# Second quads of three output projections: one 512-column matmul for the high and low parts of the input

## The chip, the cores and the metric

The kernel runs on one core of a Trainium2 chip. The metric is the device time of one execution in microseconds (us). The kernel before takes 906.71 us, the median of three runs between 906.47 and 907.17.

## The reference, cut to what matters

Two blocks of a network work on 256 tokens of width 1024, in float32. The parts that matter here:

```python
h = h + even_mixer(rmsnorm(h), ...)        # ends in concatenate([y_a, y_b]) @ w_out    (even_out)
h = h + conv_ffn(rmsnorm(h), ...)          # up0, down0
h = h + odd_mixer(rmsnorm(h), ...)         # attention, ends in y @ w_out               (qkv0, out0)
h = h + conv_ffn(rmsnorm(h), ...)          # up1, down1
h = rmsnorm(h)
h = h + mix @ w_o                          # mix: two kinds of attention                (qkv1, out1)
h = h + (gelu(gate) * val) @ w_down        # up2, down2
h = h + sigmoid(xn @ w_ple_gate) * (p @ w_ple_proj)                                   # ple
return rmsnorm(h)
```

The three output projections are products of a 256 x 1024 input with a 1024 x 1024 weight matrix, and the result is added to the residual h. Each is followed by a norm and the up projection of a feed-forward part.

## The kernel before, in words

Everything is kept transposed: 128 channels lie on the partitions, and the 256 tokens are columns. The residual `h` is 8 chunks of 128 x 256. A product in float32 accuracy is made from float32r parts: each weight w is split into a high part `wh` (w rounded, by ScalarE, line 578) and a low part `wl` (w minus `wh`, by VectorE at line 974 or GpSimd at line 516), each input x likewise into two parts that lie side by side, in `xs` (from a norm) or `ys` (from a mixer or an activation), 256 columns each. The product is wh x_high + wh x_low + wl x_high.

**Units and quads.** A unit is 128 output channels: 8 tiles of 128 x 128 weights (11 in the down phases), loaded by a DMA of SyncE into one of four slots of `raw` (line 453), rounded, split, multiplied into one of four PSUM banks `proj[:, s]`, and read out. Four units are a quad. The phases (line 59) go through their quads in order; the three output projections `even_out`, `out0` and `out1` have two quads each, so 8 units for the 8 chunks of `h`. Line 93 numbers all quads through, and semaphores count units over the whole program: `units_done` (a unit's sum is finished), `bank_read` (it is read), `hi_ready` and `lo_ready[s]` (weights rounded and split). ScalarE rounds the unit that is one quad ahead when the unit that held its slot is done (line 577). For `out0` and `out1` the weights of the first three units of the second quad are prepared early, in free room of `ys` (`early_units`, line 131, found through `split_weights`, line 393).

**Two ways to multiply on TensorE.** `unit` (line 542) issues three matmuls of 256 columns for each tile, all three into the same 256 columns of the bank; here this is called a narrow tile. `wide_unit` (line 519) issues one matmul of `wh` with both input parts, 512 columns, and one of `wl` with the high part, 256 columns, added to the second half of the bank; here a wide tile. The two halves of the bank must then be added. The up and down phases use wide tiles. `both_ys` gives both parts of `ys`, `from_ys` the two separately. All output projections use narrow tiles: their first quad is written out by hand, interleaved with the end of the mixer (lines 1840 to 1875, and 1947 and 1948), their second quad is `out_rest` (line 1621).

**The out phase on the other engines.** `residual_out` on VectorE (line 1146) does for each unit, in this order: wait for the unit, add it to its chunk of `h` (line 1154), split the weights of the unit one quad ahead (line 974), make the low part of the next norm's input (`norm_low`, line 990, after ScalarE has made the high part) and add the chunk's squares to a sum (`add_square`, line 998). For the last unit the split comes last. ScalarE's `residual_out` (line 693) rounds weights, waits for `bank_read`, and makes the high part of the norm's input (line 600) and the squares (line 595). Its `norm_root` (line 606) follows with a table load (line 607) and the root (line 614). `residual_down` on VectorE (line 1166) is the like for wide units: two additions for each unit (lines 1177 and 1178), the first inside `steps(...)`, which makes VectorE wait for its own instruction to be complete before it goes on.

**The phase behind.** `from_norm` (line 1599) starts the up phase on TensorE: seven tiles of the first unit, each waiting for its chunk's low part (`xl_ready`), seven of the second unit, then the eighth of both, the matmul of the statistics (line 1587), and the rest. So TensorE starts the next phase before the last chunk of the norm's input is there. The engines execute their own instructions in order.

Of the kernel before, what the change touches and what calls it, by code (L numbers as in the profile page):

```python
# [29 lines left out]
SEQ = 256  # L30
# [9 lines left out]
RING = 4  # L40
SLOT = HALF * P
# [46 lines left out]
def build_program(nc, streams, x_in, p_in, vectors_in, pool_in, gate_in, rel_in, onehot_in, count_in, out):  # L88
    f32, f32r = mybir.dt.float32, mybir.dt.float32r
    ALU, ACT, AX = mybir.AluOpType, mybir.ActivationFunctionType, mybir.AxisListType  # L90
    ds = bass.ds

    base, total = {}, 0
# [4 lines left out]
    quads_of = {name: quads for name, quads, _ in PHASES}  # L98
# [34 lines left out]
    def is_early(name, i, s):  # L133

        return isinstance(i, int) and (base[name] + i + 1, s) in early_units
# [10 lines left out]
    def final_unit(name, i, s):  # L146

        return isinstance(i, int) and i == quads_of[name] - 1 and s == RING - 1
# [4 lines left out]
    with ExitStack() as ctx:  # L153
        def sb(name, shape, dt=f32):
            return ctx.enter_context(nc.sbuf_tensor(name, shape, dt))

        def sem(name):
            return ctx.enter_context(nc.semaphore(name))

        h = sb("h", [P, DC, SEQ])  # L160
# [4 lines left out]
        wh = sb("wh", [P, RING, SLOT], f32r)  # L165
        wl = sb("wl", [P, RING, SLOT], f32r)
# [80 lines left out]
        proj, aux = psum[:, 0:RING, :], psum[:, RING:2 * RING, :]  # L247
# [33 lines left out]
        def squares(n, parity):  # L281

            if n == 7:
                return last_square[:, parity:parity + 1, :]
            bank = (2 if n % 2 == 0 else RING) + parity
            return psum[:, bank:bank + 1, 0:SEQ]
# [20 lines left out]
        units_done = sem("units_done")  # L307
        bank_read = sem("bank_read")
# [84 lines left out]
        def split_weights(q, s, width):  # L393

            if isinstance(q, int) and (q, s) in early_units:
                at = PAIRS * 2 * SEQ + s * 2 * DC * P
                return flat_ys[:, at:at + DC * P], flat_ys[:, at + DC * P:at + 2 * DC * P]
            return wh[:, s, 0:width], wl[:, s, 0:width]

        def unit_bank(name, i, s):  # L400

            if name == "out1" and isinstance(i, int) and i == 0 and s == RING - 1:
                return spare_bank
            return proj[:, s:s + 1, 0:SEQ]
# [6 lines left out]
        def each_quad(engine, first, end, body, steps=None, per_quad=0):  # L411


            if end - first < 2:
                for i in range(first, end):
                    body(i)
                return
            begun = steps.n if steps else 0
            with engine.Fori(first, end) as i:
                if steps:  # L420
                    steps.base, steps.n = (i - first) * per_quad + begun, 0
                body(i)
                if steps:
                    assert steps.n == per_quad, steps.n
            if steps:
                steps.base, steps.n = 0, begun + per_quad * (end - first)
# [540 lines left out]
        def _(dve):  # L967
            steps = Steps(dve, dve_step)
# [7 lines left out]
            def split_ahead(name, i, s):  # L976

                target, q = ahead(name, i, s)
                if target and s not in pool_slots(target, q):
                    split_unit(q, s, tiles_of[target])  # L980

            def phase(name, body, per_quad=0):
                last = quads_of[name] - 1
                each_quad(dve, 0, last, lambda i: body(i), steps, per_quad)
                body(last)

            def norm_low(n, m):

                dve.wait_ge(xh_ready, m + (DC * n + 1))
                nc.vector.scalar_tensor_tensor(xs[:, ds(m, 1), 1, :], h[:, ds(m, 1), :], column(VECTORS[n][0], m),  # L990
                                               xs[:, ds(m, 1), 0, :].bitcast(f32), ALU.mult, ALU.subtract).then_inc(xl_ready, 1)

            def add_square(n, m, parity):
                dve.wait_ge(square_ready, m + (DC * n + 1))
                dve.wait_ge(square_used, m + DC * n)
                if n == MID:
                    nc.vector.tensor_tensor(mid_acc[:, :], mid_acc[:, :], mid_square[:, parity, :], ALU.add)
                nc.vector.tensor_tensor(acc[:, :], acc[:, :], squares(n, parity)[:, 0, :], ALU.add).then_inc(square_used, 1)
# [67 lines left out]
            for padded, width in ((pool_u, PAD), (pool_a, PAD), (pool_b, PAD), (even_cv, TAPS - 1)):  # L1066
                last = nc.vector.memset(padded[:, 0:width], 0.0)
# [75 lines left out]
            def clear_acc():  # L1143
                steps(nc.vector.memset(acc[:, :], 0.0))

            def residual_out(name, n):
                clear_acc()

                def body(i):
                    q = i + base[name]  # L1150
                    for s in range(RING):
                        m = i * RING + s
                        dve.wait_ge(units_done, q * RING + s + 1)
                        nc.vector.tensor_tensor(h[:, ds(m, 1), :], h[:, ds(m, 1), :], unit_bank(name, i, s), ALU.add)\
                          .then_inc(bank_read, 1)
                        final = final_unit(name, i, s)
                        if not final and not is_early(name, i, s):
                            split_ahead(name, i, s)
                        dve.wait_ge(bank_read, q * RING + s + 1)
                        norm_low(n, m)  # L1160
                        add_square(n, m, s % 2)
                        if final:
                            split_ahead(name, i, s)
                phase(name, body)
# [328 lines left out]
            for i in range(quads_of["ple"]):  # L1493
                q = i + base["ple"]
                for s in range(RING):
                    m = i * RING + s
# [21 lines left out]
        def _(pe):  # L1518
            def wide_unit(q, s, inputs, tiles, start=True, stop=True, ready=None, read=None, bank=None):


                bank = proj[:, s if bank is None else bank, :]
                if tiles[0] == 0:
                    pe.wait_ge(lo_ready[s], q + 1)
                    if start and read is not None:
                        pe.wait_ge(bank_read, read)
                for n, t in enumerate(tiles):
                    if ready:
                        ready(t)
                    first, last = start and n == 0, stop and n == len(tiles) - 1  # L1530
                    w = slice(t * P, (t + 1) * P)
                    nc.tensor.matmul(bank, wh[:, s, w], inputs(t), start=first, stop=False)  # L1532
                    done = nc.tensor.matmul(bank[:, SEQ:2 * SEQ], wl[:, s, w], inputs(t)[:, 0, :], start=False, stop=last)  # L1533
                return done

            def both_xs(t):
# [24 lines left out]
            ALL = range(DC)  # L1561

            def slot_read(q, s):

                return None if isinstance(q, int) and q == 0 else q * RING + s - 3
# [9 lines left out]
            def slot_bank(s):  # L1575
                return proj[:, s, 0:SEQ]
# [15 lines left out]
            def quad_of(name, inputs):  # L1592
                def quad(i, slots=range(RING)):
                    q = i + base[name]
                    for s in slots:
                        unit(q, s, slot_bank(s), inputs, ALL, read=slot_read(q, s)).then_inc(units_done, 1)
                return quad
# [21 lines left out]
                each_quad(pe, 1, quads_of[name], quad)  # L1619

            def out_rest(name):
                each_quad(pe, 1, quads_of[name], quad_of(name, from_ys))

            def down_phase(name, ys_name):

# [14 lines left out]
            def attention(layer, name, out_name, n_norm):  # L1640
# [233 lines left out]
                for s in range(RING):  # L1874
                    out_unit(s, range(DC - 1, DC), start=False).then_inc(units_done, 1)
                out_rest(out_name)

            def tables():
# [49 lines left out]
            for j in range(1, quads_of["even_in"]):  # L1928
                for s in range(RING):
                    read = slot_read(j, s)  # L1930
                    if s == 0:

                        pe.wait_ge(pooled_in, j)
                        read = None
                    elif (j, s) == (1, 1):
                        pe.wait_ge(conv_copied, 1)
                        read = None
# [7 lines left out]
            q = base["even_out"]  # L1945
# [17 lines left out]
            for i in range(quads_of["ple"]):  # L1963
                q = i + base["ple"]
                for s in range(RING):
# [4 lines left out]
                    for t in range(PLE):  # L1970
                        w = slice((DC + t) * P, (DC + t + 1) * P)
# [18 lines left out]
            for b in range(2):  # L1990
                last = nc.tensor.matmul(last_stat[:, b:b + 1], squares(7, 1)[:, 0, b * P:(b + 1) * P], ones[:, 0:1], start=False, stop=True,
                                        skip_group_check=True)
# [3 lines left out]
            for b in range(2):  # L1996
                last = nc.tensor.matmul(last_rows[:, b * P:(b + 1) * P], last_rstd[:, b:b + 1].to_broadcast([P, P]), ident[:, :],
                                        start=True, stop=True)
# [106 lines left out]
```

## Time and profile before

| | us |
|---|---|
| median of 3 runs | 906.71 |
| lowest and highest | 906.47, 907.17 |
| the profiled execution | 907.1 |
| its span, first to last instruction | 905.4 |
| TensorE busy | 898.6 |
| VectorE busy | 670.1 |
| ScalarE busy | 572.1 |
| GpSimd busy | 243.6 |

The profile is of one execution. PE is TensorE's matmuls and PEld its weight loads, DVE is VectorE, ACT is ScalarE, POOL is GpSimd. An engine is busy while it executes at least one instruction; matmuls overlap in TensorE's pipeline, so the durations of single matmuls add up to more than its busy time. Idle time of an engine is put down to the instruction that ended it. The mean granted clock of TensorE over the span is 0.999 of full speed.

### The profile page before, as it was taken

Reading aid. Unit: us, or ns where it says so; the run is one execution under the profiler, and the core shown is the slowest. Engines: PE = TensorE matmul, PEld = TensorE weight load, DVE = VectorE, ACT = ScalarE, POOL = GpSimd, SP = SyncE. Lnnn points to the kernel's source line nnn. Section 1 sums busy time; section 2 is a strip of 40 time slices with the busy share of each in tenths; the row PEclk is TensorE's granted clock in tenths of the full one; section 3 lists DMA queues with packets and bytes.
Section 4 is the critical chain, followed back from the end, with each engine's and each line's share of the span. In section 5 each row is a group of like instructions: output and inputs, shape, how many; then the busy total and the mean of one; then the engine's idle time right before and its main releaser. Section 6 shows DMA issues by size and latency. Waiting matters only on the chain.

```text
span 905.4 us, 18274 instructions
## 1 busy us (share of the span) xinstructions
PE 898.6 (99%) x6022; PEld 814.0 (90%) x6022; DVE 670.1 (74%) x1353; ACT 572.1 (63%) x996; POOL 243.6 (27%) x130
## 2 busy tenths in 40 slices
PE   9999999999999999999999999999999999999997
PEld 8999888888898999988888888999998888888897
DVE  8987887786657756678777866788667766686566
ACT  7456776774445556577666644667658877774453
POOL 0421444420000002044443000070104988850000
PEclk9999999999999999999999999999999999999999
DMA  8545677677534434456666654444335655576521
GB/s 307 196 167 163 210 236 238 210 225 268 173 130 140 139 129 153 162 167 210 231 193 212 230 190 147 127 154 141 119 122 179 211 190 192 192 236 208 185 96 47
DMA packets 47193, 163.51 MB, mean 181 GB/s; under 512 B 5234, under 2 KB 10098, under 8 KB 47141
## 3 DMA queue, kind: packets, MB, share of 16 engines
q1 hardware_dynamic: 42336, 158.12, 53.5%
q10 hardware_dynamic: 4805, 4.70, 1.6%
q8 instruction: 32, 0.52, 0.3%
q14 instruction: 20, 0.16, 0.1%
HBM read 161.71 MB, written 3.44 MB: 182 GB/s over the span
## 4 chain that ended last, share of the span: by engine, by line
PE 95%; DVE 2%; ACT 1%; issue 1%; DVEq 0%
PE psum L1532 41%; PE psum L1533 20%; PE psum L1556 7%; PE psum L1557 7%; PE psum L1558 7%; PE psum L1679 2%; PE psum L1681 2%; PE psum L1682 2%; PE psum L1792 1%; PE psum L1894 1%; PE psum L1767 1%; PE psum L1731 1%; PE psum L1729 1%; ACT wh L578 1%; PE psum L1905 0%
## 5 line engine op out<-in xcount | busy, mean ns | idle before, releaser
L578 ACT ACTIVATE wh<-raw 128x1024 fp32r<-128x1024 f32 (+2 forms) x266 | 297.1, 1119 | 116.4 <-PE psum L1533 80.6
L1532 PE MATMUL psum<-xs,wh 128*128 128x512 f32 x1056 | 367.2, 394 | 0.0
L516 POOL TENSOR_TENSOR wl<-raw,wh 128x1024 fp32r<-128x1024 f32 (+1 forms) x86 | 209.5, 2440 | 450.7 <-ACT wh L578 449.3
L1533 PE MATMUL psum<-xs,wl 128*128 128x256 f32 x1056 | 292.7, 277 | 0.0
L974 DVE TENSOR_TENSOR wl<-raw,wh 128x1024 fp32r<-128x1024 f32 (+2 forms) x180 | 241.3, 1345 | 52.3 <-ACT wh L578 52.0
L1532 PEld LDWEIGHTS psum<-xs,wh 128*128 128x128 f32 x1056 | 198.0, 188 | 45.9
L1533 PEld LDWEIGHTS psum<-xs,wl 128*128 128x128 f32 x1056 | 198.3, 188 | 0.1
L1532 PE MATMUL psum<-ys,wh 128*128 128x512 f32 x528 | 183.2, 394 | 0.0
L1533 PE MATMUL psum<-ys,wl 128*128 128x256 f32 x528 | 146.3, 277 | 0.0
L1556 PE MATMUL psum<-xs,wh 128*128 128x256 f32 x416 | 120.3, 289 | 0.0
L1532 PEld LDWEIGHTS psum<-ys,wh 128*128 128x128 f32 x528 | 99.0, 188 | 23.0
L1558 PE MATMUL psum<-xs,wl 128*128 128x256 f32 x416 | 117.6, 283 | 0.0
L1557 PE MATMUL psum<-xs,wh 128*128 128x256 f32 x416 | 117.6, 283 | 0.0
L1031 DVE SCALAR_TENSOR_TENSOR psum<-work,vec,psum 128x256 f32<-128x256 f32 x184 | 88.7, 482 | 23.7 <-ACT psum L732 23.3
L1533 PEld LDWEIGHTS psum<-ys,wl 128*128 128x128 f32 x528 | 99.1, 188 | 0.0
L1023 DVE TENSOR_TENSOR psum<-psum,work 128x256 f32<-128x256 f32 x132 | 56.6, 429 | 40.8 <-ACT work L729 40.6
L729 ACT ACTIVATE work<-psum 128x256 f32<-128x256 f32 x132 | 50.4, 382 | 51.1 <-PE psum L1533 50.8
L1556 PEld LDWEIGHTS psum<-xs,wh 128*128 128x128 f32 x416 | 79.6, 191 | 1.6 <-issue 1.4
L1557 PEld LDWEIGHTS psum<-xs,wh 128*128 128x128 f32 x416 | 79.7, 192 | 0.1
L1558 PEld LDWEIGHTS psum<-xs,wl 128*128 128x128 f32 x416 | 79.6, 191 | 0.0
L732 ACT ACTIVATE psum<-work,vec 128x256 f32<-128x256 f32 x88 | 50.1, 569 | 36.7 <-DVE work L1014 33.7
L1014 DVE TENSOR_TENSOR work<-psum,rstd 128x256 f32<-128x256 f32 x100 | 42.1, 421 | 5.2
(239 smaller groups left out, 1230.3 us busy)
## 6 DMA issues: line engine op xcount, KB each, us to landing
raw<-in_up SPq DMA_DIRECT2D x132, 512.0 KB, 3.3
raw<-in_down SPq DMA_DIRECT2D x48, 704.0 KB, 4.2
raw<-in_qkv SPq DMA_DIRECT2D x48, 512.0 KB, 3.3
raw<-in_out SPq DMA_DIRECT2D x16, 512.0 KB, 3.4
raw<-in_even_in SPq DMA_DIRECT2D x12, 512.0 KB, 3.6
raw<-in_ple SPq DMA_DIRECT2D x8, 640.0 KB, 3.8
raw<-in_even_out SPq DMA_DIRECT2D x8, 512.0 KB, 3.6
raw<-in_even_in SPq DMA_DIRECT2D x8, 256.0 KB, 5.2
```

The lines of the kernel that those rows point to most:

```text
L516: nc.gpsimd.tensor_tensor(low, raw[:, s, 0:tiles * P], high.bitcast(f32), ALU.subtract)\
L578: nc.scalar.activation(split_weights(q, s, tiles * P)[0], raw[:, s, 0:tiles * P], ACT.Copy).then_inc(hi_ready, 1)
L729: nc.scalar.activation(high_sums[:, s % 2, :], proj[:, s, 0:SEQ], ACT.Copy).then_inc(high_copied, 1)
L732: nc.scalar.activation(target, padded[:, 2:2 + SEQ], ACT.Identity, bias=column(bias_name, chunk), scale=column(taps, chunk + 2 * chunks)). ...
L974: nc.vector.tensor_tensor(low, raw[:, s, 0:tiles * P], high.bitcast(f32), ALU.subtract).then_inc(lo_ready[s], 1)
L1023: return nc.vector.tensor_tensor(proj[:, s, 0:SEQ], proj[:, s, SEQ:2 * SEQ], high_sums[:, s % 2, :], ALU.add)
L1031: return nc.vector.scalar_tensor_tensor(out_ap, padded[:, k:k + SEQ], column(taps, chunk + k * chunks), out_ap, ALU.mult, ALU.add)
L1532: nc.tensor.matmul(bank, wh[:, s, w], inputs(t), start=first, stop=False)
L1533: done = nc.tensor.matmul(bank[:, SEQ:2 * SEQ], wl[:, s, w], inputs(t)[:, 0, :], start=False, stop=last)
L1556: nc.tensor.matmul(bank, high_w[:, w], high, start=first, stop=False)
L1557: nc.tensor.matmul(bank, high_w[:, w], low, start=False, stop=False)
L1558: done = nc.tensor.matmul(bank, low_w[:, w], high, start=False, stop=last)
```

## The change

The second quad of each output projection is computed by `wide_unit` with `both_ys`, in place of `unit` with `from_ys`: per tile one matmul of 512 columns and one of 256 in place of three of 256. `wide_unit` now takes its weights through `split_weights`, so that it finds those that were prepared early. On VectorE the addition of each unit of the second quad (`i == 1`) becomes two: the first half of the bank, a wait for that addition through `steps`, then the second half; `bank_read` is raised by the second. The first quads stay as they were.

```diff
--- before.py
+++ after.py
@@ -1151,8 +1151,12 @@
                     for s in range(RING):
                         m = i * RING + s
                         dve.wait_ge(units_done, q * RING + s + 1)
-                        nc.vector.tensor_tensor(h[:, ds(m, 1), :], h[:, ds(m, 1), :], unit_bank(name, i, s), ALU.add)\
-                          .then_inc(bank_read, 1)
+                        added = nc.vector.tensor_tensor(h[:, ds(m, 1), :], h[:, ds(m, 1), :], unit_bank(name, i, s), ALU.add)
+                        if isinstance(i, int) and i == 1:
+
+                            steps(added)
+                            added = nc.vector.tensor_tensor(h[:, ds(m, 1), :], h[:, ds(m, 1), :], proj[:, s:s + 1, SEQ:2 * SEQ], ALU.add)
+                        added.then_inc(bank_read, 1)
                         final = final_unit(name, i, s)
                         if not final and not is_early(name, i, s):
                             split_ahead(name, i, s)
@@ -1524,13 +1528,14 @@
                     pe.wait_ge(lo_ready[s], q + 1)
                     if start and read is not None:
                         pe.wait_ge(bank_read, read)
+                high_w, low_w = split_weights(q, s, SLOT)
                 for n, t in enumerate(tiles):
                     if ready:
                         ready(t)
                     first, last = start and n == 0, stop and n == len(tiles) - 1
                     w = slice(t * P, (t + 1) * P)
-                    nc.tensor.matmul(bank, wh[:, s, w], inputs(t), start=first, stop=False)
-                    done = nc.tensor.matmul(bank[:, SEQ:2 * SEQ], wl[:, s, w], inputs(t)[:, 0, :], start=False, stop=last)
+                    nc.tensor.matmul(bank, high_w[:, w], inputs(t), start=first, stop=False)
+                    done = nc.tensor.matmul(bank[:, SEQ:2 * SEQ], low_w[:, w], inputs(t)[:, 0, :], start=False, stop=last)
                 return done
 
             def both_xs(t):
@@ -1619,7 +1624,9 @@
                 each_quad(pe, 1, quads_of[name], quad)
 
             def out_rest(name):
-                each_quad(pe, 1, quads_of[name], quad_of(name, from_ys))
+                q = base[name] + 1
+                for s in range(RING):
+                    wide_unit(q, s, both_ys, ALL, read=slot_read(q, s)).then_inc(units_done, 1)
 
             def down_phase(name, ys_name):
```

## Rows read from the trace of the kernel before

**Rows 1.** The page: busy time by engine, granted clock by slice, chain by engine.

```profile
PE 898.6 (99%) x6022; PEld 814.0 (90%) x6022; DVE 670.1 (74%) x1353; ACT 572.1 (63%) x996; POOL 243.6 (27%) x130
...
PEclk9999999999999999999999999999999999999999
...
PE 95%; DVE 2%; ACT 1%; issue 1%; DVEq 0%
```

**Rows 2.** Timeline of TensorE in even_out; columns: start us, us, engine, line, instruction.

```profile
56.10 0.28 PE L1556 MATMUL psum<-ys,wh 128*128 128x256 f32 x1
...
79.02 0.19 PEld L1532 LDWEIGHTS psum<-xs,wh 128*128 128x128 f32 x1
...
79.14 0.40 PE L1532 MATMUL psum<-xs,wh 128*128 128x512 f32 x1
```

**Rows 3.** Timeline of TensorE at the start of up1.

```profile
380.69 0.40 PE L1532 MATMUL psum<-xs,wh 128*128 128x512 f32 x1
...
382.81 0.40 PE L1532 MATMUL psum<-xs,wh 128*128 128x512 f32 x1
...
386.34 0.59 PE L1587 MATMUL psum<-acc,ones 128*128 128x256 f32 x2
```

**Rows 4.** Line 1533 in down0: duration ns min/median/max, first and last start.

```profile
L1533 PE MATMUL psum<-ys,wl x176: 274/277/280, 201.9 to 262.6; 128*128 128x256 f32 x176
```

**Rows 5.** Timeline of VectorE in out0, second quad.

```profile
376.10 0.41 DVE L1154 TENSOR_TENSOR h<-h,psum 128x256 f32<-128x256 f32 x1
...
376.43 1.22 DVE L974 TENSOR_TENSOR wl<-raw,wh 128x1024 fp32r<-128x1024 f32 x1
...
378.29 0.41 DVE L1154 TENSOR_TENSOR h<-h,psum 128x256 f32<-128x256 f32 x1
...
380.49 0.41 DVE L1154 TENSOR_TENSOR h<-h,psum 128x256 f32<-128x256 f32 x1
...
381.95 0.47 DVE L990 SCALAR_TENSOR_TENSOR xs<-h,vec,xs 128x256 fp32r<-128x256 f32 x1
...
382.68 0.41 DVE L1154 TENSOR_TENSOR h<-h,psum 128x256 f32<-128x256 f32 x1
...
383.74 0.48 DVE L990 SCALAR_TENSOR_TENSOR xs<-h,vec,xs 128x256 fp32r<-128x256 f32 x1 [0.65 <-ACT xs L600]
```

**Rows 6.** Timeline of VectorE and TensorE at the start of up2.

```profile
682.32 0.40 PE L1532 MATMUL psum<-xs,wh 128*128 128x512 f32 x1
...
683.76 0.48 DVE L990 SCALAR_TENSOR_TENSOR xs<-h,vec,xs 128x256 fp32r<-128x256 f32 x1
...
684.45 0.40 PE L1532 MATMUL psum<-xs,wh 128*128 128x512 f32 x1
```

**Rows 7.** Timeline of VectorE in even_out, third unit of the second quad.

```profile
77.61 1.23 DVE L974 TENSOR_TENSOR wl<-raw,wh 128x1024 fp32r<-128x1024 f32 x1 [0.60 <-ACT wh L578]
...
78.75 0.48 DVE L990 SCALAR_TENSOR_TENSOR xs<-h,vec,xs 128x256 fp32r<-128x256 f32 x1
```

**Rows 8.** Timeline of VectorE in the down phases, first and last of 24 pairs.

```profile
213.51 0.41 DVE L1177 TENSOR_TENSOR h<-h,psum 128x256 f32 x1
214.03 0.42 DVE L1178 TENSOR_TENSOR h<-h,psum 128x256 f32 x1
...
866.11 0.42 DVE L1177 TENSOR_TENSOR h<-h,psum 128x256 f32<-128x256 f32 x1 [0.23 <-PE psum L1533]
866.63 0.42 DVE L1178 TENSOR_TENSOR h<-h,psum 128x256 f32<-128x256 f32 x1
```

**Rows 9.** Timeline at the end: TensorE released by VectorE.

```profile
896.47 0.42 DVE L998 TENSOR_TENSOR acc<-acc,work 128x256 f32<-128x256 f32 x1
...
896.95 0.52 PEld L1986 LDWEIGHTS psum<-ones,acc 128*128 128x128 f32 x4 [0.53 <-DVE acc L998]
```

**Rows 10.** Timeline of ScalarE at the start of up1.

```profile
384.91 1.28 ACT L607 ACT_TABLE_LOAD   x1
...
386.97 0.48 ACT L614 ACTIVATE work<-psum,eps 128x256 f32<-128x256 f32 x1 [0.78 <-PE psum L1587]
```

## The prediction

> **What bounds the kernel now.** I read the page first. TensorE is busy for 99% of the span, and the chain that ended last is 95% TensorE [rows 1]. Time is therefore saved by giving TensorE less to do, and lost by whatever makes it wait; work on another engine costs nothing until TensorE waits for it. The durations of single matmuls (0.28 us for 256 columns, 0.40 for 512 [rows 2]) overlap each other, so they can't be summed. I went to the timeline of TensorE for the pace from start to start. A narrow tile is three matmuls of 256 columns: the 64 tiles of even_out start at 56.10 and end at 79.14 us [rows 2], which is 23.04 / 64 = 0.360 us per tile. A wide tile is one matmul of 512 columns and one of 256. The 16 wide tiles that follow directly on narrow ones in up1 run from 380.69 to 386.34 us, 5.65 / 16 = 0.353 us per tile [rows 3]; the 176 wide tiles of down0 run at (262.6 - 201.9) / 175 = 0.347 us [rows 4].
>
> Then I read VectorE around the same places, since the change gives it more to do. In out0 the residual additions of the second quad start at 376.10, 378.29, 380.49 and 382.68 us [rows 5]: 2.19 us apart, back to back, with no idle time, while TensorE delivers a unit every 8 x 0.360 = 2.88 us. VectorE came into this quad behind. TensorE had finished the last unit when up1 began, at 380.69 [rows 3], and VectorE took it up at 382.68, 2.0 us late.
>
> **What TensorE waits for next** is the order of up1: it takes tiles 0 to 6 of its first unit at once, and each tile wants the low part of that chunk of the norm (line 990). Tile 6 wants chunk 6, which comes from the third unit of the out quad. Its low part ends at 381.95 + 0.47 = 382.42, and TensorE starts tile 6 at 382.81 [rows 3, 5]: a margin of 0.39 us. In out1 it ends at 683.76 + 0.48 = 684.24 and tile 6 starts at 684.45 [rows 6]: 0.21 us. In even_out it ends at 78.75 + 0.48 = 79.23, and tile 6 is due at 79.14 + 6 x 0.353 = 81.26 [rows 2, 7]: 2.03 us.
>
> **What the change removes.** 96 tiles (8 tiles x 4 units x 3 projections) go from three matmuls to two. If they run at the pace of wide tiles that follow narrow ones, each saves 0.360 - 0.353 = 0.007 us: 0.22 us per projection, 0.66 in all. If they run at down0's pace, 0.013 us each: 0.42 per projection, 1.25 in all, and the first 16 tiles of each up phase may then keep that pace too, another 3 x 16 x 0.006 = 0.3. The bounds of the gain are thus 0.66 and 1.55 us. I take the low one, since the second quads follow directly on a narrow first quad, as at the start of up1 [rows 3].
> TensorE's clock is granted in full, 2.4 GHz, in every slice of the span [rows 1], so the clock gives nothing back. The Trainium skill (TensorE: Matmul & The Clock Gate, section Back-to-back issue gap) puts a warm matmul at its columns over 2.4 GHz plus about 2.5 ns. By that rule an estimate would be 327.5 ns for a narrow tile and 325 for a wide one, 2.5 ns saved each, 0.24 us in all. The trace doesn't agree: its tiles take 360 and 347 to 353 ns.
>
> **What it adds.** 12 additions on VectorE, four in each second quad. The nearest rows are the two additions of the down phases, which have the same operands and the same wait between them: 213.51 to 214.03 and 866.11 to 866.63 us [rows 8]. All 24 such pairs start 0.51 to 0.53 us apart. The wait for the engine's own step lets the first one (0.42 us) drain. So each unit grows by 0.52 us, from 2.19 to 2.71. The lower bound is 0.33 us, the distance from an addition to the next independent instruction (376.10 to 376.43 [rows 5]). Behind this wait stand the split of the next phase's unit, the low part of the norm, the sum of squares and the next unit's addition; ScalarE's norm work waits for the same counter, bank_read, which now rises after the second addition. No DMA, no split and no rounding is moved. The waits for weights are far off: the split of up1's first unit is done at 376.43 + 1.22 = 377.65, 3 us before TensorE wants it [rows 3, 5].
>
> **Where it lands.** Three additions stand ahead of chunk 6: 3 x 0.52 = 1.56 us.
> In out0 VectorE has no idle time between them to absorb any of it. The low part of chunk 6 ends at 382.42 + 1.56 = 383.98. TensorE, restarted by a semaphore, loads weights 0.06 us after the releasing instruction ends (896.47 + 0.42 = 896.89 to 896.95 [rows 9]) and starts its matmul 0.12 us after the load begins (79.02 to 79.14 [rows 2]). Tile 6 starts at 383.98 + 0.18 = 384.16 instead of 382.81: **1.35 us lost**. The 0.22 us saved in this quad only makes TensorE arrive earlier and wait longer.
> In out1: 684.24 + 1.56 + 0.18 = 685.98 instead of 684.45: **1.53 us lost**, the saving swallowed as before.
> In even_out there are 2.03 us of margin less 0.22, and VectorE is idle for 0.60 us in the unit of chunk 6, waiting for ScalarE's weights [rows 7], which takes up part of the 1.56. No wait: **0.22 us saved**.
> The last chunk has one addition more. In out0 its low part started at 383.74 and took 0.48 [rows 5]; it now ends at 384.22 + 4 x 0.52 = 386.30. TensorE has 8 tiles left from 384.16 before it wants it, until 384.16 + 8 x 0.35 = 386.96: no second wait. The statistics matmul moves from 386.34 to 387.69 with TensorE; ScalarE's table load, in line behind chunk 7, ends at 384.91 + 1.28 + 2.08 = 388.27, and the root that started 0.63 us after the statistics (386.97) is due at 388.32 [rows 3, 10]. It is just in time, and I cost it at nothing.
> Sum: 1.35 + 1.53 - 0.22 = +2.66 us. The profiled execution was 907.1 us with a span of 905.4, 0.4 us above the median of 906.71, so it would be 909.8, and the median about 909.3 us. Low end: additions at 0.33 us (0.57 less in out0 and in out1), the fast pace in even_out (0.2) and in the up tiles (0.3) leave about +1.0, 907.7. High end: a second wait of some tenths behind the late last chunk or the late root in each of the two, about +3.7, 910.4. Both ends lie above the time before.
>
> **The rivals.**
> A. *VectorE has room, so TensorE's saving is all that shows.* For it: 2.71 us per unit is still less than the 2.82 (8 x 0.353) that TensorE takes, and VectorE is idle for a quarter of the span [rows 1]. The point from which it decides is the low part of chunk 6, at TensorE's arrival less 0.18 us. If VectorE kept up there, nothing would be lost and 0.66 to 1.55 us saved: about 905.6 us. Against it: the margins of 0.39 and 0.21 us are smaller than a single addition, and VectorE enters the quad behind and without idle time. Chance 0.07. This gain can't reach 0.2%.
> B. *The wait comes, but the additions cost little.* At about 0.33 us each with the fast pace everywhere the loss is some 1 us: 907.7 us. For it: the second addition could overlap the first more than in down. Against it: 24 pairs say otherwise. Chance 0.15.
> C. *The last chunk or the root becomes a second wait.* With 0.05 us of margin at the root and 0.66 at the last chunk, ScalarE's longer line behind chunk 7 could hold the first banks of up1 and up2. TensorE writes these again about 5 us later, so most is hidden; 0.5 us each would give 910.3 us. Chance 0.08.
> That the change doesn't do what it says can hardly be: the second quad is written out with a constant index, so the branch with the second addition is taken.
>
> **How the numbers follow.** The forecast, a wait at tile 6 in out0 and out1 and none in even_out, has 0.70. A measurement of this kernel can tell about 0.2%, 1.8 us, from no change: slower means over 908.5 us, faster under 904.9. The forecast at 909.3 lies above that line, but with some spread; nearly nine tenths of its 0.70 are past it, all of C too; A and B are within 0.2%. I give slower 0.70, same 0.27, faster 0.03. The range 907.6 to 910.4 leaves out A and a little at each end.
>
> **What would show it.** In the profile of the changed kernel: in out0 and out1 TensorE idle for about 1.5 us ahead of the seventh tile of the first up unit, released by line 990's instruction on VectorE, and none in even_out; the additions of the second quads 2.71 us apart in out0 and out1; two starts 0.52 us apart within each; 32 wide tiles in about 11.3 us in each second quad (at the fast pace 11.1). Wrong would be: no gap at tile 6, a gap in even_out, or a gap at the last tile or at the banks of the second up quad.

## The result, and the profile after

The changed kernel takes 910.86 us (median of 6 runs, 910.60 to 912.14), the kernel before 906.79 us in the same comparison. The ratio is 1.0047, with a 95% interval from 1.0034 to 1.0059: slower, and slower than the top of the predicted range by 0.46 us. The profiled execution (910.63 us) has a span of 908.9 us, 3.5 us more than before. The medians differ by 4.07 us; the other 0.5 us is that the profiled execution of before (907.1 us) lay 0.3 above its median and that of the changed kernel 0.2 below. All that follows explains the 3.5.

The page of the changed kernel, its span, its busy times and its chain by engine:

```profile
span 908.9 us, 18094 instructions
...
PE 898.4 (99%) x5926; PEld 813.2 (89%) x5926; DVE 674.7 (74%) x1365; ACT 572.2 (63%) x996; POOL 244.3 (27%) x130
...
PE 90%; DVE 5%; ACT 2%; issue 2%; DMA 1%; SPq 0%; DVEq 0%; ACTq 0%
```

TensorE is busy for 0.2 us less than in [rows 1] and the span is 3.5 us longer: what came on top is time in which TensorE is idle, within the program or at its start and end. The chain is no longer 95% TensorE, since it now passes through VectorE and the first loads. To see where the time lies, I compared the same points of both timelines of TensorE. First the changed kernel: the first wide tile of even_out, the statistics of up0, tile 6 and the statistics of up1, the same two of up2, and the last matmuls (columns: start us, us, engine, line, instruction, idle time before it and what ended it):

```profile
68.27 0.40 PE L1537 MATMUL psum<-ys,wh 128*128 128x512 f32 x1
...
85.23 0.59 PE L1592 MATMUL psum<-acc,ones 128*128 128x256 f32 x2
...
384.30 0.49 PE L1537 MATMUL psum<-xs,wh 128*128 128x512 f32 x1 [1.08 <-DVE xs L990]
...
384.75 0.40 PE L1537 MATMUL psum<-xs,wh 128*128 128x512 f32 x1
...
387.88 0.38 PE L1592 MATMUL psum<-acc,ones 128*128 128x256 f32 x1
...
687.21 0.49 PE L1537 MATMUL psum<-xs,wh 128*128 128x512 f32 x1 [1.26 <-DVE xs L990]
...
690.78 0.38 PE L1592 MATMUL psum<-acc,ones 128*128 128x256 f32 x1
...
902.21 0.68 PE L2004 MATMUL psum<-ident,last_rstd 128*128 128x128 f32 x4
```

The kernel before at the same points that [rows 3] doesn't hold: the first statistics, those of up0 and up2, and the last matmuls:

```profile
19.20 0.60 PE L1587 MATMUL psum<-acc,ones 128*128 128x256 f32 x2
...
84.79 0.38 PE L1587 MATMUL psum<-acc,ones 128*128 128x256 f32 x1
...
687.98 0.38 PE L1587 MATMUL psum<-acc,ones 128*128 128x256 f32 x1
...
899.42 0.69 PE L1997 MATMUL psum<-ident,last_rstd 128*128 128x128 f32 x4
```

| stretch | before us | after us | difference |
|---|---|---|---|
| start to the first statistics | 19.20 | 19.85 | +0.65 |
| to the statistics of up0 | 65.59 | 65.38 | -0.21 |
| to the statistics of up1 (wait at tile 6) | 301.55 | 302.65 | +1.10 |
| to the statistics of up2 (wait at tile 6) | 301.64 | 302.90 | +1.26 |
| to the last matmuls | 211.44 | 211.43 | -0.01 |
| to the end of the span | 5.98 | 6.69 | +0.71 |
| sum | 905.4 | 908.9 | +3.5 |

The differences at up0, up1 and up2 are those that were predicted, as -0.22, +1.35 and +1.53. Start and end, together 1.36 us, were not in the forecast at all.

**The two waits.** The waits of TensorE put them down to the instruction that was named (columns: waited for, us in total, times, longest):

```profile
PE psum L1537 <- DVE xs L990: 2.3, 2, 1.3
```

The timeline of VectorE in out0, to be laid beside [rows 5]: the two additions of the fifth unit, its split, the next two units' first additions, and chunk 6's low part:

```profile
376.55 0.41 DVE L1154 TENSOR_TENSOR h<-h,psum 128x256 f32<-128x256 f32 x1
...
377.00 0.42 DVE L1158 TENSOR_TENSOR h<-h,psum 128x256 f32<-128x256 f32 x1
...
377.34 1.22 DVE L974 TENSOR_TENSOR wl<-raw,wh 128x1024 fp32r<-128x1024 f32 x1
...
379.20 0.41 DVE L1154 TENSOR_TENSOR h<-h,psum 128x256 f32<-128x256 f32 x1
...
381.85 0.41 DVE L1154 TENSOR_TENSOR h<-h,psum 128x256 f32<-128x256 f32 x1
...
383.77 0.48 DVE L990 SCALAR_TENSOR_TENSOR xs<-h,vec,xs 128x256 fp32r<-128x256 f32 x1
```

The units are 2.65 us apart (376.55, 379.20, 381.85), not the 2.19 of before. The second addition starts 0.45 us behind the first, where 0.52 was expected from [rows 8]. The low part of chunk 6 ends at 383.77 + 0.48 = 384.25, and TensorE takes tile 6 at 384.30, 0.05 us later and not 0.18. Both terms were somewhat too large: 3 x 0.07 + 0.13 = 0.34 us. The first tile behind a wait takes 0.45 us to the next start (384.30 to 384.75), 0.10 more than usual, and the nine tiles after it run at (387.88 - 384.75) / 9 = 0.348 us, the fast pace, which gives half of that back.

ScalarE at the start of up1, to be laid beside [rows 10]: the table load ends at 388.46 and the root starts at 388.51, 0.63 us behind the statistics at 387.88, so it is in time, as the prediction had it.

```profile
387.18 1.28 ACT L607 ACT_TABLE_LOAD   x1
...
388.51 0.47 ACT L614 ACTIVATE work<-psum,eps 128x256 f32<-128x256 f32 x1
```

**The start.** ScalarE's first instruction waits for a small DMA of scale vectors. In the kernel before it starts at 3.95 us:

```profile
3.95 0.91 ACT L624 ACTIVATE xs<-h,vec 128x256 fp32r<-128x256 f32 x2 [0.41 <-DMA vec<-in_vectors]
```

In the changed kernel it waits 1.6 us longer, and the first statistics follow 0.65 us later than before. It is not this load alone: the first weights (`raw<-in_even_in`, 256 KB each) take 6.9 us from issue to landing in the page of the changed kernel, 5.2 in that of before.

```profile
5.54 0.91 ACT L624 ACTIVATE xs<-h,vec 128x256 fp32r<-128x256 f32 x2 [2.00 <-DMA vec<-in_vectors]
...
19.85 0.38 PE L1592 MATMUL psum<-acc,ones 128*128 128x256 f32 x1
```

**The end.** The DMA view of the last microseconds, of the kernel before and of the changed one (columns: what, times, KB each, median us from issue to landing):

```profile
out<-h SPq DMA_DIRECT2D x3, 256.0 KB, 2.1
...
out<-h SPq DMA_DIRECT2D x2, 128.0 KB, 1.9
```

```profile
out<-h SPq DMA_DIRECT2D x3, 256.0 KB, 2.7
...
out<-h SPq DMA_DIRECT2D x2, 128.0 KB, 2.0
```

VectorE's last instructions and the stores' issues keep their places relative to the last matmuls (0.45 us from one to the other in both), but the larger stores take 2.7 us to land in place of 2.1. Nothing in the diff touches a load or a store. The page of before lists 32 packets on queue q8, whose kind is "instruction"; the changed kernel has one fewer:

```profile
q8 instruction: 31, 0.51, 0.2%
```

These packets don't stand in the way of the first loads themselves: in the DMA views of both kernels and of experiment 8 none of them falls in the first 12 us. The number is used below only as a mark of how long the program is.

### The profile page after: what moved, and what is told of

Same layout as the page of the kernel before. It is cut to its first block, busy times and chain, and to the rows that moved or that the text cites. A ratio compares the mean times of both kernels' runs of the same rounds, so it can differ in the third digit from the quotient of the medians.

```text
span 908.9 us, 18094 instructions
## 1 busy us (share of the span) xinstructions
PE 898.4 (99%) x5926; PEld 813.2 (89%) x5926; DVE 674.7 (74%) x1365; ACT 572.2 (63%) x996; POOL 244.3 (27%) x130
## 4 chain that ended last, share of the span: by engine, by line
PE 90%; DVE 5%; ACT 2%; issue 2%; DMA 1%; SPq 0%; DVEq 0%; ACTq 0%
PE psum L1537 40%; PE psum L1538 21%; PE psum L1561 6%; PE psum L1562 6%; PE psum L1563 6%; PE psum L1686 2%; PE psum L1688 2%; PE psum L1689 2%; PE psum L1799 1%; DVE wl L974 1%; ACT wh L578 1%; DMA h<-in_x 1%; PE psum L1774 1%; DVE acc L998 1%; PE psum L1738 1%
## 5 line engine op out<-in xcount | busy, mean ns | idle before, releaser
L1537 PE MATMUL psum<-ys,wh 128*128 128x512 f32 x576 | 200.3, 392 | 0.0
L1538 PE MATMUL psum<-ys,wl 128*128 128x256 f32 x576 | 161.6, 281 | 0.0
L1537 PEld LDWEIGHTS psum<-ys,wh 128*128 128x128 f32 x576 | 107.9, 187 | 23.6
L1538 PEld LDWEIGHTS psum<-ys,wl 128*128 128x128 f32 x576 | 109.1, 189 | 0.0
L600 ACT ACTIVATE xs<-h,vec 128x256 fp32r<-128x256 f32 (+1 forms) x48 | 24.4, 508 | 34.3 <-DVE h L1158 13.6
```

The source lines that it names most:

```text
L1537: nc.tensor.matmul(bank, high_w[:, w], inputs(t), start=first, stop=False)
L1538: done = nc.tensor.matmul(bank[:, SEQ:2 * SEQ], low_w[:, w], inputs(t)[:, 0, :], start=False, stop=last)
```

## The experiments

**Theory T:** the additions on VectorE, which starts the second quad behind, make tile 6 late, as predicted; start and end are slower because TensorE's program has become shorter and its code lies otherwise. **Rivals:** start and end vary from execution to execution; the wide matmuls or the use of both halves of a bank cause them; or the second quads are too slow on VectorE whatever happens in the first. In this section "the middle" is the time from the first statistics to the last matmuls, read in each timeline as above: 880.22 us before, 882.36 changed.

**1 and 2. Both kernels again, unchanged.**

> The changed kernel, unchanged. Of the 3.5 us by which its span is longer, its trace shows 0.65 us ahead of the first statistics, -0.21 in even_out, +1.10 at up1's tile 6, +1.26 at up2's, and 0.70 behind the last matmuls. Theory (the waits at tile 6 are the change, start and end are the execution's): 909 to 911 us, and the waits again 1.0 to 1.3 us, while start and end differ from the first profile by some tenths. Rival (the changed program starts and ends later every time): start and end as in the first profile, 910.9 us.

> The kernel before, unchanged, for a second look at its start and end. Theory: 906.8 us, with the first statistics matmul within a few tenths of 19.2 to 19.85 us in either kernel. Rival (start and end belong to the program): first statistics at 19.20 us and the last matmuls to the end of the span as in the first profile.

Measured: the changed kernel 910.73 us, the kernel before 906.62. First statistics at 19.79 and 19.34 us, the middle 882.39 and 880.25, the end 6.7 and 5.9 us behind the last matmuls. So the slow start and end are the program's and come again. The rival of c_after was right, and my expectation that they would differ by tenths was wrong.

**3. One addition only.**

```diff
-                        if isinstance(i, int) and i == 1:
-                            steps(added)
-                            added = nc.vector.tensor_tensor(h[:, ds(m, 1), :], h[:, ds(m, 1), :], proj[:, s:s + 1, SEQ:2 * SEQ], ALU.add)
```

> The changed matmuls with the first of the two additions alone: the low parts' sum, the second half of the bank, is left out of the residual in the second quads. Theory (the additions make the waits): no wait at tile 6 in up1 and up2 or one of some hundredths, 0.66 us less than before at the slow pace, 906.1 us, plus what start and end give (up to 1.4). Rival (the wide matmuls themselves delay something, their banks or their clock): still 1.5 us or more above before at tile 6.

Measured: 908.16 us (ratio 1.0016, 1.0007 to 1.0024). The middle is 879.72 us, 0.50 less than before: without the second addition nothing is lost, and the wide matmuls save somewhat less than the 0.66 that was expected of their slow pace. Yet the kernel is slower than before. In the profiled execution its first statistics come at 21.21 us, and its stores land late as in the changed kernel:

```profile
out<-h SPq DMA_DIRECT2D x3, 256.0 KB, 2.8
```

The start is worse than that of the changed kernel because TensorE was granted only half of its clock for a while. Before that it had waited 1.06 us for a small load; in the changed kernel that wait is 0.2 us. This execution took 909.41 us, 1.25 more than the median, which suggests that the lowered clock belongs to it and not to most executions. (The second line is the window from 8 to 10 us: us, busy time and count of PE, PEld, DVE, ACT and POOL, granted clock, DMA share, GB/s.)

```profile
6.73 1.03 PE L1884 MATMUL psum<-qkv 33*18 33x512 f32 x2 [1.06 <-DMA qkv<-in_rel]
...
8.00:10.00 2.00, 1.75 (x8) 1.76 (x9) 1.91 (x5) 1.58 (x4) 0.00 (x0) 0.50 1.05 395
```

**4. The additions alone, on the narrow kernel.**

```diff
-                        nc.vector.tensor_tensor(h[:, ds(m, 1), :], h[:, ds(m, 1), :], unit_bank(name, i, s), ALU.add)\
-                          .then_inc(bank_read, 1)
+                        added = nc.vector.tensor_tensor(h[:, ds(m, 1), :], h[:, ds(m, 1), :], unit_bank(name, i, s), ALU.add)
+                        if isinstance(i, int) and i == 1:
+                            steps(added)
+                            added = nc.vector.tensor_tensor(h[:, ds(m, 1), :], h[:, ds(m, 1), :], unit_bank(name, i, s), ALU.add)
+                        added.then_inc(bank_read, 1)
```

> The matmuls of the kernel before, but the first half of the bank is added a second time in the second quads, with the same wait between (so the residual gets the sum twice there). Theory: up1's and up2's tile 6 start at the same point behind VectorE as in the changed kernel, 1.1 and 1.3 us late, and even_out saves nothing: 2.4 us above before, 909.2 us. Rival (the additions alone are hidden): within 0.5 us of before.

Measured: 909.32 us, ratio 1.0027 (1.0017 to 1.0037), as T expected. The middle is 882.64 us, 2.42 above before; start (19.31) and end (5.9 us) are those of before. The waits of TensorE:

```profile
PE psum L1535 <- DVE xs L990: 1.9, 2, 1.1
```

They are 0.2 us shorter for each than in the changed kernel, since narrow tiles bring TensorE to tile 6 later. So the two waits come from the additions alone, and start and end do not.

**5. Two narrow matmuls per tile.** The product with the input's low part is left out in the second quads; no tile is wide.

```diff
 def out_rest(name):
-    each_quad(pe, 1, quads_of[name], quad_of(name, from_ys))
...
+    for t in ALL:
+        nc.tensor.matmul(slot_bank(s), high_w[:, w], ys[:, t, 0, :], start=t == 0, stop=False)
+        last = nc.tensor.matmul(slot_bank(s), low_w[:, w], ys[:, t, 0, :], start=False, stop=t == DC - 1)
```

> The kernel before with two narrow matmuls for each tile of the second quads (the product with the input's low part is left out there): 96 instructions pairs fewer, as in the changed kernel, but none wide. If the length of the program makes the slow start and end: first statistics later than 19.4 us and the end more than 6.3 us behind the last matmul. If the wide matmuls or the halves of the bank do: 19.2 to 19.35 and 5.9 to 6.0 us. TensorE saves up to 11.5 us in the second quads and VectorE then binds there.

Measured (a single execution): 907.2 us, first statistics at 20.11 us, the end 6.7 us behind the last matmuls, 31 packets on q8. A shorter program without wide matmuls has the slow start and end too; so neither the wide matmuls nor the bank halves are needed for them. The middle is only 1.57 us shorter than before although TensorE's work is 11.5 us less: it now waits for VectorE in all three places.

**6. A float32 matmul ahead of the wide quads.**

```diff
 q = base[name] + 1
+nc.tensor.matmul(psum[:, 7, 0:P], ones[:, :], ones[:, :], start=True, stop=True)
 for s in range(RING):
```

> The changed kernel with one float32 matmul of 128 columns ahead of each wide second quad. In both kernels wide tiles run at 0.353 us behind narrow ones and at 0.347 behind the float32 matmuls of the statistics. If such a matmul is what ends the slower pace: the 32 tiles of the second quad take 11.1 us in place of 11.3. If it is the statistics' place or the phase: 11.3 us as before.

Measured (a single execution): 912.43 us, most of the difference to the changed kernel at the start (21.43 us, with the granted clock at 0.50 between 10 and 12 us) and 0.2 in the middle. TensorE's timeline at the start of even_out's second quad:

```profile
69.85 0.39 PE L1628 MATMUL psum<-ones 128*128 128x128 f32 x2
...
69.99 0.48 PE L1537 MATMUL psum<-ys,wh 128*128 128x512 f32 x1
...
70.42 0.39 PE L1537 MATMUL psum<-ys,wh 128*128 128x512 f32 x1
...
70.77 0.40 PE L1537 MATMUL psum<-ys,wh 128*128 128x512 f32 x1
...
71.13 0.40 PE L1537 MATMUL psum<-ys,wh 128*128 128x512 f32 x1
...
71.48 0.40 PE L1537 MATMUL psum<-ys,wh 128*128 128x512 f32 x1
```

After the first tile the starts are again 0.35 to 0.36 us apart, and the second half of the quad runs at 0.353. So a float32 matmul by itself does not end the slow pace, although it comes with a first tile of 0.43 us, much like the one behind a wait.

**7. 96 small matmuls at the end of TensorE's program.**

```diff
 last.then_inc(last_spread, 1)
+for _ in range(96):
+    nc.tensor.matmul(proj[:, 0, 0:32], wh[:, 0, 0:P], xs[:, 0, 0, 0:32], start=True, stop=True)
```

> The changed kernel with 96 small matmuls added behind everything that TensorE has to do, so that its program holds as many instructions as before. Theory (the first loads and the last stores are slower because the program got shorter and lies otherwise): first statistics back at 19.2 to 19.35 us, end of the span 5.9 to 6.0 us behind the last needed matmul, 1.3 to 1.4 us less than the changed kernel, 909.4 us. Rival (start and end go with something else in the change): start at 19.8 us, 910.8 us.

Measured: 920.47 us, not the 909.4 that T expected. The 96 matmuls took 18.3 us, far longer than the stores that they were to hide behind, so this total and this end say nothing. The start does: first statistics at 19.35 us, ScalarE's first instruction at 3.93, 32 packets on q8, as before the change.

**8. 192 waits that are always satisfied.**

```diff
+def filler(t):
+    for _ in range(2):
+        pe.wait_ge(ones_ready, 1)
-wide_unit(q, s, both_ys, ALL, read=slot_read(q, s)).then_inc(units_done, 1)
+wide_unit(q, s, both_ys, ALL, ready=filler, read=slot_read(q, s)).then_inc(units_done, 1)
```

> The changed kernel with two waits that are always satisfied ahead of each wide tile of the second quads, 192 in all, to bring TensorE's program back to about its former length without giving the engine work. If the length makes the slow start and end: first statistics at 19.2 to 19.4 us, the end of the span 5.9 to 6.0 us behind the last matmul, the waits at tile 6 unchanged, 909.0 to 909.5 us. If not: 910.8 us. If the waits themselves slow the wide tiles, it shows as more than 11.4 us for a second quad.

Measured: 909.03 us, ratio 1.0024 (1.0014 to 1.0034). The middle is 882.51 us, within 0.15 of the changed kernel. The stores and queue q8 are those of before, and the start is back too; the first statistics come even 0.4 us earlier than the 19.20 of before:

```profile
3.89 0.91 ACT L624 ACTIVATE xs<-h,vec 128x256 fp32r<-128x256 f32 x2 [0.35 <-DMA vec<-in_vectors]
...
18.81 0.38 PE L1592 MATMUL psum<-acc,ones 128*128 128x256 f32 x1
```

```profile
out<-h SPq DMA_DIRECT2D x3, 256.0 KB, 2.1
```

```profile
q8 instruction: 32, 0.52, 0.2%
```

The same work in a longer program is 1.8 us faster. 909.03 is also near the 909.3 of the prediction, which had left start and end alone.

**9. One satisfied wait ahead of each tile, in place of two** (against experiment 8).

```diff
-    for _ in range(2):
+    for _ in range(1):
```

> The changed kernel with one satisfied wait ahead of each wide tile of the second quads in place of two, 96 in all, so half of the missing length. If start and end go with the length by degrees: first statistics near 19.4 us, the last stores half as late, 909.9 us. If it is a step (how the program lies): either like the changed kernel, 19.8 us or more and 910.8 us, or like the one with 192 waits, 18.8 to 19.3 us and 909.0 us.

Measured: 910.74 us, first statistics at 19.95 us, the larger stores 2.8 us to landing, the end 6.7 us behind the last matmuls:

```profile
q8 instruction: 31, 0.51, 0.2%
```

The expectation calls this half of the missing length. The pages don't bear that out; these are their first lines for experiments 8 and 9:

```profile
span 907.3 us, 18190 instructions
...
span 909.0 us, 18094 instructions
```

The changed kernel has 18094 instructions too. So 192 waits added 96 instructions, and 96 waits added none: of two waits ahead of a tile only one counts as an instruction of its own. Experiment 9 therefore didn't test half the length. It is a control: satisfied waits that make the program no longer leave start and end as slow as they were. Whether the effect of the length is a step or a slope stays open. No profile lies between the two groups: the seven with 18190 instructions or more have 32 packets on q8 and their first statistics at 18.8 to 19.4 us, the seven with 18106 or fewer have 31 and 19.8 to 21.4. For a step speaks that 96 added instructions brought back the whole start and end, where the page counts 96 matmuls and 96 weight loads fewer than before; but how many instructions of the program these are isn't shown.

**10. VectorE adds a unit ahead in the first quads of out0 and out1,** on the changed kernel. The body of the addition becomes `add_unit(s)`:

```diff
+begun = isinstance(i, int) and i == 0 and name != "even_out"
+if begun:
+    add_unit(0)
 for s in range(RING):
     m = i * RING + s
+    if not begun:
+        add_unit(s)
+    elif s < RING - 1:
+        add_unit(s + 1)
     final = final_unit(name, i, s)
```

> The changed kernel, and in the first quads of out0 and out1 VectorE adds a unit to the residual ahead of the norm of the unit before, in place of waiting 0.65 us for ScalarE each time. Theory (the backlog from the first quad is what makes the additions late): VectorE reaches the fifth unit some 1.7 us earlier, no wait at tile 6 in up1 and up2, 0.66 us less than before between the first statistics and the last matmuls, 907.5 to 908.2 us with start and end as in the changed kernel. Rival (the second quad itself is too slow for VectorE): waits of 1 us and more remain, 910 us.

Measured: 907.94 us, ratio 1.0014 (1.0005 to 1.0023). No wait at tile 6; the middle is 879.29 us, 0.93 less than before. That is 0.27 more than expected, which isn't explained; 0.51 of the 0.93 lie in the stretch to the statistics of up2. What is left above the kernel before is the start and the end (6.7 us). The profiled execution (908.86 us, 0.9 above the median) has its first statistics at 21.11 us, again with a lowered clock behind a wait of 1.2 us for the same small load.

**11. The same order on the kernel before.**

> The kernel before with the additions of the first quads of out0 and out1 a unit ahead, nothing else. TensorE does not wait there, so it should give nothing: 906.8 us, with VectorE at the fifth unit of out0 1.7 us earlier. More than 0.5 us either way would mean that the order on VectorE acts elsewhere too.

Measured: 906.79 us, ratio 0.9998 (0.9989 to 1.0007), the middle 880.25 us. Counted from the first statistics, VectorE reaches the fifth unit of out0 1.8 us earlier (1.7 expected), but TensorE wasn't waiting there, and it gives nothing.

**12. Both remedies on the changed kernel:** the addition a unit ahead, and the 192 satisfied waits.

> The same filling on the kernel whose first quads of out0 and out1 add a unit ahead. If the change is worth its 0.22 us per projection once VectorE's backlog and the program's length are both dealt with: no wait at tile 6, 0.6 to 0.8 us below before, 906.0 to 906.3 us. If one of them remains: 907 us and more.

Measured: 906.01 us (905.79 to 906.73), beside 906.85 for the kernel before: ratio 0.9991, interval 0.9982 to 1.0000. The middle is 879.58 us, 0.64 less than before. VectorE in the first quad of out0, with its residual additions and low parts, and the fifth unit:

```profile
369.80 0.41 DVE L1154 TENSOR_TENSOR h<-h,psum 128x256 f32<-128x256 f32 x1
...
370.13 0.48 DVE L990 SCALAR_TENSOR_TENSOR xs<-h,vec,xs 128x256 fp32r<-128x256 f32 x1
...
370.86 0.41 DVE L1154 TENSOR_TENSOR h<-h,psum 128x256 f32<-128x256 f32 x1
...
371.19 0.48 DVE L990 SCALAR_TENSOR_TENSOR xs<-h,vec,xs 128x256 fp32r<-128x256 f32 x1
...
373.92 0.41 DVE L1154 TENSOR_TENSOR h<-h,psum 128x256 f32<-128x256 f32 x1
```

From the second unit on, additions and low parts now follow each other without a wait for ScalarE. Counted from the first statistics, the fifth unit starts at 373.92 - 19.03 = 354.89 us, in place of 376.10 - 19.20 = 356.90: 2.0 us earlier, 0.2 of them from even_out. TensorE at tile 6, tile 7 and the statistics of up1:

```profile
382.57 0.40 PE L1547 MATMUL psum<-xs,wh 128*128 128x512 f32 x1
...
382.93 0.40 PE L1547 MATMUL psum<-xs,wh 128*128 128x512 f32 x1
...
385.76 0.59 PE L1602 MATMUL psum<-acc,ones 128*128 128x256 f32 x2
```

There is no gap. This is the only version with the wide second quads that isn't slower than the kernel before. The gain of 0.8 us in the medians is at the edge of what the measurement can tell.

## Why the prediction was wrong, point by point

**The saving on TensorE: right.** 32 wide tiles that follow narrow ones keep the slow pace of 0.353 us, and even_out gained 0.21 us (0.22 forecast). In out0 and out1 nothing of it shows. The rule that the prediction took from the Trainium skill (TensorE: Matmul & The Clock Gate, section Back-to-back issue gap) is given there for a single isolated matmul, and not for a stream of weight loads and matmuls as here; its estimate for even_out would be 0.08 us. The trace goes with the rows and not with it.

**The waits at tile 6: right in place, number and cause, a little too large.** Forecast 1.35 and 1.53 us, measured 1.10 and 1.26. The term for one addition was 0.52 us from the down phases and measured 0.45; the restart of TensorE was 0.18 and measured 0.05. Experiments 3 and 4 take the two parts of the change apart, and only the additions bring the waits. Experiment 10 shows what they rest on: VectorE's idle time in the first quad, 0.65 us per unit in which it waits for ScalarE. The prediction saw the backlog that comes of it, but not where it comes from.

**even_out without a wait, the last chunk and the root in time: right.** No gap appears in any of these places. Rival C didn't happen, nor did A and B.

**Start and end: this is the step that failed.** The sum of the prediction, "1.35 + 1.53 - 0.22 = +2.66 us", was put straight on the time of the whole kernel, with the words "No DMA, no split and no rounding is moved". That start and end stay as they are was assumed and had no term and no bound. They cost 0.65 + 0.71 = 1.36 us in the profile. With the wait terms at their measured size the sum is +2.15, and 2.15 + 1.36 = 3.5 us is the span's difference. The direction was right; the range, whose top stood at 910.4, had no room for this. Shown is that they go with the length of TensorE's program and not with the work in it: the changed kernel with 96 more instructions that do nothing (experiment 8) has both as before, and with 96 small matmuls at its end (7) the start too; waits that add no instruction change nothing (9), and a shorter program without wide matmuls has both slow (5). How the length reaches the first loads and the last stores isn't shown. The number of instruction packets goes with it in every profile, but it may just count the length; the placing of code or buffers in memory was not tried apart from it.

## What to carry to other kernels

An engine that the page shows idle for a quarter of the time can still be the one that is late: before moving work onto it, look at where it is behind, take the margin of the next thing that waits for it, and compare it with the added work that stands ahead. Here the margins were 0.39 and 0.21 us and the added work 3 x 0.45 = 1.35. If the backlog comes from idle time further up, reordering there (adding a unit ahead) takes the loss away: here the 2.4 us of the two waits at tile 6, where the change itself saves 0.6 us. Without the change the reordering gave nothing (experiment 11). And where less than half a per cent is at stake, a change of the program's length is a change too: compare the first and the last microseconds of both traces, and keep a term for them in the range.

## What the runs showed that was not expected

- First loads and last stores depend on the length of a program that doesn't contain them. The first small load was waited for until 3.9 to 4.0 us in all profiles with 32 packets on the instruction queue and until 5.1 to 6.0 us in all with 31; the larger stores landed in 2.1 us in the first group (2.3 in experiment 7, beside its filling) and in 2.7 to 2.8 in the second.
- A late start can cost twice. In the profiled execution of experiment 3 TensorE waited 1.06 us for a small load and then had a granted clock of 0.50, its lower level of 1.2 GHz, between 8 and 10 us, and the first statistics came at 21.2 instead of 19.8 us. The profiles of experiments 6 and 10, with waits of 1.3 and 1.2 us for the same load, have such a stretch too; no other profile has either.
- Wide tiles have two paces, 0.353 and 0.347 us, that hold for long stretches of the same instructions. They run at the slow one when they follow narrow tiles without a break, at the fast one behind the statistics and behind the wait at tile 6 (0.348). A single float32 matmul doesn't switch them. What the statistics and the wait have in common, and whether it can be had for less than it gives, is open.
- Two dependent additions start 0.52 us apart in the down phases and 0.45 us apart in the out phases, with the same operands and the same kind of wait. In the profile of the changed kernel both are there side by side: 0.44 to 0.45 for all 12 pairs of the second quads, 0.52 to 0.53 for 23 of the 24 pairs of the down phases. Why is open.
